# Three fox tiles per chunk in the chunk loop of a two-block transformer kernel, x as the first transfer, and fewer matmul pieces per attention unit

## The chip, the cores and the metric

One core of one Trainium2 chip. The metric is device time in microseconds (us) of one execution. The kernel before takes 821.96 us, the median of 3 runs (821.44 to 823.97).

## The reference, cut to what matters

Two transformer blocks run one after the other on x, 256 tokens of width 1024, all in float32. The change lies in the front half of the first block:

```python
cond = silu(c)
mod = cond @ w_ada + b_ada                    # 6 * 1024 columns
sh1, sc1, g1, sh2, sc2, g2 = split(mod, 6)
h = rms(x, ln1_g) * (1 + sc1) + sh1
u = h @ w_in                                  # 4616 columns
fq, fk, fv, fg, dq, dk, dv = split(u, ...)    # 512, 512, 512, 8, 512, 512, 512 * 2 ...
fox_out  = fox_attention(rms(fq), rms(fk), fv, log_sigmoid(fg + b_f))   # 8 heads of 64
diff_out = diff_attention(rms(dq), rms(dk), dv, lam, slopes)            # 4 heads of 2 x 64
x = x + g1 * (concat(fox_out, diff_out) @ w_out)
```

After it come the feed-forward part of the first block and the whole second block, which the change leaves as they are.

## The kernel before, in words

**One order for all engines.** `plan` (L81) writes out a single list of steps, ORDER. Each engine's program walks that list and executes its own share of each step, in that order, and waits on semaphores for the others. So a step that waits on ScalarE or VectorE holds back everything that stands behind it in the list on that engine. The sync engine (SP) issues the weight transfers from the same list: every `split`, `chunk` and `ada` step has one slab of weights, which lands in one of RAW = 5 slots (L761 to L803). A slot is issued again only when the work on the step five places earlier has freed it (L778 to L786).

**Pieces and splits.** A matmul in float32 is made of three products: a weight slab is cut by a `split` step into a high part (ScalarE, `whi`, L1182) and a low part (VectorE, `wlo`, L1400), and a `piece` is one chunk of 128 rows of the contraction for one tile of 512 output columns: 3 products for each of the 2 token tiles, 6 matmuls (L873 to L875). A tile of `w_in` takes 8 pieces and then an `evac` step: ScalarE copies it out of PSUM (L1335) and, for the first two tiles of fox and of diff, squares it (L1340); VectorE then sums the squares (L1730). There are three fox tiles (q, k, v) and three diff tiles. Where a piece is the first of its slab, `plan` places all splits up to two slabs ahead just before it (L266 to L269).

**The chunk loop.** h can't be made before the adaptive shift and scale are known, so the first part of `w_ada` is taken in 8 chunks of 128 columns for shift and for scale. For chunk j: `rows` (16 matmuls, L916, of the landed chunk with cond), a copy of the row by ScalarE (L1192), `xT` (transposes of the normalised x, L927), `col` (the row turned to columns, 4 entries in a line of the trace, L936), then on VectorE the affine step (L1431, L1432, L1437), and `part0`: high part of h on ScalarE (L1196), low part on VectorE (L1443). Chunk j of h then feeds piece j of every tile of `w_in`. Before the change the loop multiplies two tiles, fox q and fox k, per chunk: the order is piece j of tile 0, `rows` of chunk j+2, piece j of tile 1, then `xT`, `col`, `part0` of chunk j+2 and the split of slab j+2. A slab is 128 rows of 1024 columns. Rows sit in PSUM banks 4 and 5, the transposed x in banks 6 and 7. Fox v follows after the loop as an ordinary tile, behind `fgate` (the forget gates, L1010 to L1013). Then come `logf`, `cum` (L1021) and `heads` 0 (L1034).

**The attention part.** `attention` (L124) writes 8 units here, 4 fox and 4 diff. Unit u puts `scores` of unit u+1 first (L1050, L1058), then `probsT` u (the probabilities transposed, L1079), `heads` u+2, and `values` u (L1109, L1110), and fills the places between them with pieces and `ada` steps (L961, the rest of `w_ada`) from a list called `tail`. BETWEEN (L72) says how many for each place. ScalarE executes the exponentials (L1273), the high parts of the heads (L1264, L1265) and the copies of the transposed probabilities (L1282); VectorE the bias and maximum (L1611, L1612, L1629), the normalisation (L1634 to L1653) and the low parts of the heads (L1588, L1590). The scores of the second head of a unit and the transposed probabilities share PSUM bank 6, so `probsT` u waits for VectorE to have read the scores of u+1.

The places that the change touches:

```python
BETWEEN = {"fox": (2, 1, 2, 1, 2), 1: (2, 1, 2, 1, 1), 2: (3, 1, 1, 0, 1), 3: (2, 0, 2, 0, 1),
           "diff": (2, 0, 1, 0, 1), 7: (1, 0, 1, 0, 2), ...
# unit u: scores u+1, [0] pieces, probsT (u,0), [1] pieces, heads u+2, [2] pieces, probsT (u,1), [3] pieces, values u, [4] pieces
# probsT (u,1) is there for fox units only; [3] likewise
order += [("scores", 0), ("heads", 1), ("lam", 0)] + tail[:3]
```

Of the kernel before, what the change touches and what calls it, by code (L numbers as in the profile page):

```python
# [71 lines left out]
BETWEEN = {"fox": (2, 1, 2, 1, 2), 1: (2, 1, 2, 1, 1), 2: (3, 1, 1, 0, 1), 3: (2, 0, 2, 0, 1),  # L72
           "diff": (2, 0, 1, 0, 1), 7: (1, 0, 1, 0, 2),
# [267 lines left out]
def build(nc, A, out):  # L341

    ctx = ExitStack()
    with ctx:
# [266 lines left out]
        def home(s):  # L611

            return (s // 2 % SPL, s % 2) if s < KC else ((s - KC // 2) % SPL, 0)

        def split_view(t, s):
            slot, half = home(s)
            return t[:, slot, half * 2 * W:half * 2 * W + SLABS[s]["chunks"] * SLABS[s]["cols"]]

# [194 lines left out]
        def _(pe):  # L813
# [41 lines left out]
            for it in ORDER:  # L855
                kind, i = it
                if kind == "piece":
# [1092 lines left out]
```

## Time and profile before

| | us |
|---|---|
| median of 3 runs | 821.96 |
| the profiled execution, its own time | 823.87 |
| span of its trace | 822.1 |
| TensorE (PE) busy | 785.4 |
| VectorE (DVE) busy | 461.3 |
| ScalarE (ACT) busy | 392.6 |
| GpSimd (POOL) busy | 59.2 |

The profiled execution took 1.8 us more than the span of its trace and 1.9 us more than the median. A time in the trace is counted from the span's start. The duration of a matmul in the trace is pipelined (the next starts before it ends), so what a group of matmuls takes is read from the start of one to the start of the next. PEld is the load of the stationary operand, "issue" an idle time for which the profile shows no releaser, and PEclk the granted share of TensorE's clock.

### The profile page before, as it was taken

To read this page: it belongs to the slowest core of one execution; us is meant where nothing else is said; L and a number is where in the kernel's file an instruction comes from. 1 tells how busy PE (TensorE), PEld (TensorE's weight loads), DVE (VectorE), ACT (ScalarE), POOL (GpSimd) and SP (SyncE) were. 2 spreads that over 40 slices of the span, in tenths; PEclk is the share of its full clock that TensorE was granted. 3 is DMA by queue.
4 is the path that set the end of the run, shared out by engine and by line. 5 is a ranking of instruction groups with operands and counts; after the bars stand their busy time and mean duration, and the time that the engine had idled before them with its cause. 6 is when DMAs were issued, how large, how long until landed. Compare 5 with 4: busy or idle time off the path is not lost.

```text
span 822.1 us, 10250 instructions
## 1 busy us (share of the span) xinstructions
PE 785.4 (96%) x3963; PEld 623.7 (76%) x3963; DVE 461.3 (56%) x607; ACT 392.6 (48%) x546; POOL 59.2 (7%) x66
## 2 busy tenths in 40 slices
PE   4898899998999999999999999999999999999995
PEld 2567676566888889788888887777888888888884
DVE  3466676646565556364574445556566565544364
ACT  3255656644344334353644456664464545335252
POOL 2014020000000000000281000000010000000001
PEclk9999999998999999999999999999999999999998
DMA  9997336895555356555758464333555645564601
GB/s 274 294 364 268 104 109 254 335 377 175 196 194 188 122 153 232 202 179 186 255 198 307 154 204 155 103 103 104 159 184 183 184 174 188 174 202 153 202 29 51
DMA packets 86433, 157.67 MB, mean 192 GB/s; under 512 B 5134, under 2 KB 23783, under 8 KB 84338
## 3 DMA queue, kind: packets, MB, share of 16 engines
q1 hardware_dynamic: 84562, 151.16, 55.2%
q0 software_dynamic: 1776, 5.85, 2.3%
q8 instruction: 32, 0.52, 0.3%
q14 instruction: 15, 0.12, 0.0%
q10 hardware_dynamic: 48, 0.01, 0.0%
HBM read 155.94 MB, written 1.07 MB: 191 GB/s over the span
## 4 chain that ended last, share of the span: by engine, by line
PE 85%; DVE 4%; SPq 3%; issue 3%; ACT 2%; DMA 2%; POOL 0%; DVEq 0%; POOLq 0%; ACTq 0%
PE PS L873 25%; PE PS L875 24%; PE PS L874 24%; PE PS L999 2%; DMA raw<-in_w_ada 2%; PE PS L961 1%; PE PS L1109 1%; PE PS L1050 1%; PE PS L1079 1%; ACT whi L1182 1%; SPq L803 1%; DVE wlo L1400 1%; PE PS L1034 1%; SPq L791 1%; SPq L776 1%
## 5 line engine op out<-in xcount | busy, mean ns | idle before, releaser
L1400 DVE TENSOR_TENSOR wlo<-raw,whi 128x2048 fp32r<-128x2048 f32 (+1 forms) x126 | 275.2, 2185 | 197.4 <-ACT whi L1182 170.5
L1182 ACT ACTIVATE whi<-raw 128x2048 fp32r<-128x2048 f32 (+1 forms) x126 | 227.2, 1804 | 154.0 <-PE PS L875 154.0
L873 PE MATMUL PS<-whi,hT 128*128 128x512 f32 (+1 forms) x704 | 280.8, 399 | 2.1 <-issue 1.4
L875 PE MATMUL PS<-whi,hT 128*128 128x512 f32 (+1 forms) x704 | 273.4, 388 | 0.0
L874 PE MATMUL PS<-wlo,hT 128*128 128x512 f32 (+1 forms) x704 | 273.2, 388 | 0.0
L873 PEld LDWEIGHTS PS<-whi,hT 128*128 128x128 f32 x704 | 133.7, 190 | 32.3 <-issue 7.5
L875 PEld LDWEIGHTS PS<-whi,hT 128*128 128x128 f32 x704 | 133.6, 190 | 27.5
L874 PEld LDWEIGHTS PS<-wlo,hT 128*128 128x128 f32 x704 | 134.0, 190 | 24.1
L873 PE MATMUL PS<-whi,hidT 128*128 128x512 f32 x216 | 84.9, 393 | 0.0
L875 PE MATMUL PS<-whi,hidT 128*128 128x512 f32 x216 | 84.1, 389 | 0.0
L874 PE MATMUL PS<-wlo,hidT 128*128 128x512 f32 x216 | 84.1, 389 | 0.0
L874 PEld LDWEIGHTS PS<-wlo,hidT 128*128 128x128 f32 x216 | 40.6, 188 | 8.5 <-issue 0.2
L873 PEld LDWEIGHTS PS<-whi,hidT 128*128 128x128 f32 x216 | 40.6, 188 | 8.5 <-issue 0.2
L875 PEld LDWEIGHTS PS<-whi,hidT 128*128 128x128 f32 x216 | 40.5, 188 | 8.4
L1273 ACT ACTIVATE sc<-sc,nmax 128x128 f32<-128x128 f32 x64 | 28.5, 446 | 33.2 <-DVE nmax L1629 33.0
L1837 POOL TENSOR_TENSOR nss<-nss 128x2 f32<-128x2 f32 x4 | 0.8, 190 | 571.1 <-ACT mod L1172 352.7
L1238 ACT ACTIVATE hidT<-PS 128x512 fp32r<-128x512 f32 x27 | 14.7, 597 | 43.1 <-PE PS L999 43.1
L1540 DVE SCALAR_TENSOR_TENSOR hidT<-PS,hidT 128x512 fp32r<-128x512 f32 x27 | 17.4, 686 | 22.1 <-ACT hidT L1238 22.1
L916 PE MATMUL PS<-raw,cond 128*32 128x256 f32 x128 | 10.3, 447 | 12.5 <-DMA raw<-in_w_ada 12.4
L1365 ACT ACTIVATE hid<-PS 128x1024 f32<-128x1024 f32 x8 | 8.2, 1029 | 24.0 <-PE PS L875 24.0
L1079 PEld LDWEIGHTS PS<-con,sc 128*128 128x128 f32 x84 | 9.9, 140 | 11.4 <-issue 9.4
L1050 PEld LDWEIGHTS PS<-kT,qT 64*128 64x128 f32 x192 | 12.4, 186 | 7.8 <-issue 6.5
(230 smaller groups left out, 669.5 us busy)
## 6 DMA issues: line engine op xcount, KB each, us to landing
raw<-in_w_in SPq DMA_DIRECT2D x36, 1024.0 KB, 5.2
raw<-in_w_ff SPq DMA_DIRECT2D x32, 1024.0 KB, 5.2
raw<-in_w_ada SPq DMA_DIRECT2D x16, 1024.0 KB, 6.4
raw<-in_w_gate SPq DMA_DIRECT2D x10, 1024.0 KB, 5.2
raw<-in_w_up SPq DMA_DIRECT2D x10, 1024.0 KB, 5.1
raw<-in_w_down SPq DMA_DIRECT2D x10, 1024.0 KB, 5.1
raw<-in_w_ada SPq DMA_DIRECT2D x16, 512.0 KB, 7.1
raw<-in_w_out SPq DMA_DIRECT2D x8, 1024.0 KB, 5.0
```

The lines of the kernel that those rows point to most:

```text
L873: pe.matmul(o, ah, wh, start=(k == 0), stop=False)
L874: pe.matmul(o, ah, wl, start=False, stop=False)
L875: return pe.matmul(o, al, wh, start=False, stop=end)
L916: last = pe.matmul(PS[r:r + 32, b, 0:256], cond32[:, k, :], raw[:, slot, k * 256:(k + 1) * 256], start=k < 4, stop=k >= 4)
L999: last = pe.transpose(PS[:, b, o:o + P], src[:, t, c * P:(c + 1) * P], ident)
L1050: last = pe.matmul(PS[:, 5 + n, c0:c1], qT[r, slot, qp, t * P:(t + 1) * P], kT[r, slot, kp, 0:c1 - c0], start=m == 0, stop=m == 2 and not ...
L1079: last = pe.transpose(PS[:, probs_bank(u, n), m * P:(m + 1) * P], src[:, n, c:c + P], ident)
L1182: act.activation(split_view(whi, i), slab_view(raw, slot, i), ACT.Copy).then_inc(hi_made, 1)
L1238: act.activation(hi.rearrange("p c s -> p (c s)"), PS[:, b, :], ACT.Copy, scale=1.0 if gain is None else gain).then_inc(turn_hi, 1)
L1273: act.activation(sc[:, n, c0:c1], sc[:, n, c0:c1], ACT.Exp, bias=nmax[:, a, t:t + 1], scale=-1.0, accum_out=lsum[:, a, t:t + 1]).then_inc( ...
L1400: dve.tensor_tensor(split_view(wlo, i), slab_view(raw, slot, i), whole(split_view(whi, i)), ALU.subtract).then_inc(lo_made, 1)
L1540: dve.scalar_tensor_tensor(out=lo.rearrange("p c s -> p (c s)"), in0=PS[:, b, :], scalar=1.0 if gain is None else gain, in1=hi.rearrange(" ...
```

## The change

The chunk loop multiplies all three fox tiles for each chunk, from slabs of 128 rows by 1536 columns. Fox v has its own two PSUM banks (4 and 5), and the rows move to the banks of the transposed x (6 and 7). `rows` of a chunk now come one chunk ahead of the pieces instead of two: rows j+1, piece j of tile 0, then `xT`, `col`, the split and `part0` of chunk j+1, then piece j of tiles 1 and 2. At the end of the loop the last pieces go tile by tile, so that tiles 0, 1 and 2 are evacuated one after another. `fgate`, `unit` and `logf` follow, and then the whole first diff tile, with one split after its fourth piece, `cum` after the fifth, `heads` 0 after the sixth, and behind its `evac` a split, `scores` 0, `heads` 1 and `lam`. Then two pieces of the second diff tile, and the attention part with 5, 5, 5, 4, 3, 3, 3, 3 pieces in its units, where it had 8, 7, 6, 5, 4, 4, 4, 3. The split buffers are one ring of three slabs from the start. The two small transfers for cond (`crow`, `con`) go from the queue of SP to that of ScalarE, so x is the first that SP issues.

```diff
-BETWEEN = {"fox": (2, 1, 2, 1, 2), 1: (2, 1, 2, 1, 1), 2: (3, 1, 1, 0, 1), 3: (2, 0, 2, 0, 1),
-           "diff": (2, 0, 1, 0, 1), 7: (1, 0, 1, 0, 2),
+BETWEEN = {"fox": (2, 1, 1, 0, 1), 3: (1, 1, 1, 0, 1), "diff": (1, 0, 1, 0, 1),
            "moba": (2, 0, 1, 0, 1), 8: (2, 0, 1, 0, 0), 15: (2, 1, 1, 1, 1)}
...
-    fox = [tile("fox", n, KC, "h") for n in range(2)]
+    fox = [tile("fox", n, KC, "h") for n in range(3)]
...
-    order += [("cond", 0), ("chunk", 0), ("sums0", 0), ("norm", 0), ("rows", 0), ("early", 0), *early, ("xT", 0), *column(0)]
-    order += [*rows(1), ("xT", 1), *early, *column(1)]
+    order += [("cond", 0), ("chunk", 0), ("sums0", 0), ("norm", 0), ("rows", 0), ("early", 0), ("xT", 0), ("col", 0), *early,
+              ("part0", 0)]
     for j in range(KC):
-        slabs.append(dict(weight="w_in", row=j * P, chunks=1, col=0, cols=2 * W))
-        pair = [("piece", dict(T=fox[n], k=j, slab=j, off=n * W, first=n == 0, last=n == 1)) for n in range(2)]
-        if j < KC - 2:
-            order += [pair[0], *rows(j + 2), pair[1], ("xT", j + 2), *column(j + 2), *early]
-            order += {KC - 4: [("setup", 0)], KC - 3: early + [("relbias", 0)]}.get(j, [])
-        elif j == KC - 2:
-            order += [pair[0], *early, ("vectors", 0)]
-            second = pair[1]
+        slabs.append(dict(weight="w_in", row=j * P, chunks=1, col=0, cols=3 * W))
+        step = [("piece", dict(T=fox[n], k=j, slab=j, off=n * W, first=n == 0, last=n == 2)) for n in range(3)]
+        if j < KC - 1:
+            order += rows(j + 1) + step[:1] + [("xT", j + 1), ("col", j + 1), *early, ("part0", j + 1)]
+            if j < KC - 2:
+                order += step[1:]
+                order += [("setup", 0)] if j == KC - 3 else []
+            else:
+                order += [("relbias", 0)]
+                held = step[1:]
         else:
-            order += [pair[0], ("evac", fox[0]), second, pair[1], ("evac", fox[1])]
+            for n in range(3):
+                order += (held[n - 1:n] if n else early + [("vectors", 0)]) + step[n:n + 1] + [("evac", fox[n])]
     order += early + [("fgate", 0), ("unit", 0), ("logf", 0), ("unit", 1)]
-    now = whole("fox", 2, "w_in", 2 * W, "h")
-    order += insert(now, (4, early), (5, [("cum", 0)]), (6, [("heads", 0)]))
     tail = []
     for n in range(3):
         tail += whole("diff", n, "w_in", 3 * W + FOX + n * W, "h")
-    tail = insert(tail, (11, [("unit", 2)]), (20, [("unit", 3)]), (23, ada[8:10]))
+    tail = insert(tail, (4, early), (5, [("cum", 0)]), (6, [("heads", 0)]), (9, early + [("scores", 0), ("heads", 1), ("lam", 0)]),
+                  (11, [("unit", 2)]), (20, [("unit", 3)]), *[(20 + j, [ada[8 + j]]) for j in range(6)])
     wo = [tile("w_out", n, KC, "mix") for n in range(2)]
     fill = slab(wo[0], "w_out", 0, 0) + slab(wo[1], "w_out", W, 0)
-    tail += insert(fill, *[(j, [ada[10 + j]]) for j in range(8)])
-    order += [("scores", 0), ("heads", 1), ("lam", 0)] + tail[:3]
-    tail = tail[3:]
+    tail += insert(fill, *[(2 * j, [ada[14 + j]]) for j in range(4)])
+    ahead = tail.index(("unit", 2))
+    order += tail[:ahead]
+    tail = tail[ahead:]
...
         def home(s):
-            return (s // 2 % SPL, s % 2) if s < KC else ((s - KC // 2) % SPL, 0)
+            return s % SPL
...
         def slabs_under(s):
-            slot, half = home(s)
-            under = [e for e in range(s) if home(e)[0] == slot and (e >= KC or s >= KC or home(e)[1] == half)]
-            return under[-1] + 1 if under else 0
+            return max(0, s - SPL + 1)
...
         def bank0(T):
-            return 2 * (T % 2)
+            return 2 * T if T < 3 else 2 * ((T - 3) % 2)
...
-            sp.dma_start(crow[:, :], A["c"].rearrange("a (r q) -> (a r) q", q=P)).then_inc(cond_in, 16)
-            sp.dma_start(con[:, C_ID:C_ID + P], A["constants"][:, C_ID:C_ID + P]).then_inc(cond_in, 16)
...
-                    b = 4 + i % 2
+                    b = chunk_bank(i)
...
                 elif kind == "xT":
                     b = chunk_bank(i)
-                    take(b)
+                    pe.wait_ge(row_in, i + 1)
...
-                    take(5)
-                    pe.transpose(PS[:, 5, 0:V_ALL], vec[:, :], ident[0:V_ALL, 0:V_ALL]).then_inc(vec_ps, 1)
+                    take(7)
+                    pe.transpose(PS[:, 7, 0:V_ALL], vec[:, :], ident[0:V_ALL, 0:V_ALL]).then_inc(vec_ps, 1)
...
+            act.dma_start(crow[:, :], A["c"].rearrange("a (r q) -> (a r) q", q=P)).then_inc(cond_in, 16)
+            act.dma_start(con[:, C_ID:C_ID + P], A["constants"][:, C_ID:C_ID + P]).then_inc(cond_in, 16)
```

## Rows read from the trace of the kernel before

**Rows 1.** The page: busy time of each engine.
```profile
PE 785.4 (96%) x3963; PEld 623.7 (76%) x3963; DVE 461.3 (56%) x607; ACT 392.6 (48%) x546; POOL 59.2 (7%) x66
```

**Rows 2.** Waits of PE, 0 to 222 us: total us, times, longest.
```profile
PE PS L916 <- DMA raw<-in_w_ada: 12.4, 6, 7.4
```

**Rows 3.** Windows: stretch, us, busy per engine, PEclk, DMA share, GB/s.
```profile
40.00:50.00 10.00, 9.61 (x76) 6.42 (x68) 5.29 (x11) 3.80 (x7) 0.00 (x0) 1.00 1.14 331
50.00:60.00 10.00, 8.62 (x43) 6.43 (x40) 8.07 (x12) 7.30 (x8) 0.45 (x1) 1.00 1.04 386
...
73.30:76.80 3.50, 3.50 (x12) 2.76 (x12) 3.20 (x3) 2.08 (x3) 0.00 (x0) 0.51 0.25 91
```

**Rows 4.** Timeline of chunk steps: start us, us, engine line, operation, idle before.
```profile
34.35 1.07 PE L916 MATMUL PS<-raw,cond 128*32 128x256 f32 x16 [1.47 <-DMA raw<-in_w_ada]
...
44.13 1.07 PE L916 MATMUL PS<-raw,cond 128*32 128x256 f32 x16 [0.22 <-DMA raw<-in_w_ada]
45.13 0.50 PE L873 MATMUL PS<-whi,hT 128*128 128x512 f32 x1
47.20 0.48 PE L873 MATMUL PS<-whi,hT 128*128 128x512 f32 x1
47.76 0.54 DVE L1437 TENSOR_SCALAR aff<-PS,AB 128x256 f32<-128x256 f32 x1
49.01 1.07 PE L916 MATMUL PS<-raw,cond 128*32 128x256 f32 x16 [0.17 <-DMA raw<-in_w_ada]
```

**Rows 5.** Groups by line and form, 10 to 56 us: busy us, mean ns.
```profile
L1400 DVE TENSOR_TENSOR wlo<-raw,whi 128x1024 fp32r<-128x1024 f32 x8 | 9.8, 1226 | 6.7 <-ACT whi L1182 6.7
L1182 ACT ACTIVATE whi<-raw 128x2048 fp32r<-128x2048 f32 x1 | 1.9, 1894 | 0.0
```

**Rows 6.** Timeline, issue of x, end of the loop, the gates.
```profile
1.66 0.43 SPq L763 DMA_DIRECT2D x<-in_x  x1
...
56.03 0.47 PE L873 MATMUL PS<-whi,hT 128*128 128x512 f32 x1 [1.39 <-issue]
...
60.22 2.51 PE L825 MATMUL PS<-hT,wfgs 128*72 128x256 f32 x20
...
62.92 0.19 PEld L873 LDWEIGHTS PS<-whi,hT 128*128 128x128 f32 x1
...
68.17 0.47 DVE L1554 TENSOR_SCALAR fgt<-PS,bf 72x256 f32<-72x256 f32 x1
...
72.60 0.26 PE L1021 MATMUL PS<-con,fgt 8*128 8x8 f32 x2 [2.57 <-DVE fgt L1563]
```

**Rows 7.** Timeline of the first scores, of PE and DVE.
```profile
80.64 0.29 DVE L1611 TENSOR_SCALAR mcum<-con,cumq 128x128 f32<-128x128 f32 x1 [2.68 <-issue]
...
85.44 0.55 PE L1050 MATMUL PS<-kT,qT 64*128 64x128 f32 x6 [0.17 <-DVE kT L1590]
...
90.01 0.28 DVE L1611 TENSOR_SCALAR mcum<-con,cumq 128x128 f32<-128x128 f32 x1
92.52 0.52 PE L1079 MATMUL PS<-con,sc 128*128 128x128 f32 x3 [2.74 <-DVE nmax L1629]
92.96 1.90 ACT L1182 ACTIVATE whi<-raw 128x2048 fp32r<-128x2048 f32 x1
```

**Rows 8.** Timeline of ACT and DVE around the evac of the first diff tile.
```profile
99.27 1.03 ACT L1335 ACTIVATE tok<-PS 128x1024 f32<-128x1024 f32 x1 [2.73 <-PE PS L875]
101.46 1.93 ACT L1182 ACTIVATE whi<-raw 128x2048 fp32r<-128x2048 f32 x1
103.48 2.29 DVE L1400 TENSOR_TENSOR wlo<-raw,whi 128x2048 fp32r<-128x2048 f32 x1 [1.02 <-ACT whi L1182]
```

**Rows 9.** Timeline of a diff unit on DVE and ACT, and the end of attention.
```profile
148.39 0.38 ACT L1300 ACTIVATE tok<-PS 128x256 f32<-128x256 f32 x1 [1.22 <-PE PS L825]
149.32 0.19 ACT L1305 ACTIVATION_READ_ACCUMULATOR sq<-tok 128x1 f32 x1
...
172.38 1.09 PE L999 MATMUL PS<-con,tok 128*128 128x128 f32 x8
```

More of the change, by code:

```diff
@@ L611, in home @@
         def home(s):
-            return (s // 2 % SPL, s % 2) if s < KC else ((s - KC // 2) % SPL, 0)
+            return s % SPL
         def split_view(t, s):
-            slot, half = home(s)
-            return t[:, slot, half * 2 * W:half * 2 * W + SLABS[s]["chunks"] * SLABS[s]["cols"]]
+            return t[:, home(s), 0:SLABS[s]["chunks"] * SLABS[s]["cols"]]
         def slabs_under(s):
-            slot, half = home(s)
-            under = [e for e in range(s) if home(e)[0] == slot and (e >= KC or s >= KC or home(e)[1] == half)]
-            return under[-1] + 1 if under else 0
+            return max(0, s - SPL + 1)
         def landed(eng, it):
@@ L862, in _ @@
                         pe.wait_ge(lo_made, s + 1)
-                    if k == 0 and T >= 2:
-                        for ready in tile_readers(T - 2):
+                    if k == 0 and tile_under(T) >= 0:
+                        for ready in tile_readers(tile_under(T)):
                             pe.wait_ge(*ready)
+                    if (T, k) == (2, 0):
+                        take(4, 5)
                     operand_ready(T, k)
@@ L892, in _ @@
                         last.then_inc(gemm_done, 1)
-                    elif (T, k) == (0, KC - 1):
+                    elif T < 2 and k == KC - 1:
                         last.then_inc(first_done, 1)
+                    if (T, k) == (2, KC - 1):
+                        reader[4] = reader[5] = tile_readers(T)
                 elif kind == "cond":
@@ L935, in _ @@
                     for a in range(2):
-                        last = pe.matmul(PS[:, chunk_bank(i), S + a:S + a + 1], row_of(i)[:, a * P:(a + 1) * P], sel[:, :],
+                        last = pe.matmul(PS[:, chunk_bank(i), a:a + 1], row_of(i)[:, a * P:(a + 1) * P], sel[:, :],
                                          start=True, stop=True)
                     last.then_inc(col_ps, 1)
+                    reader[chunk_bank(i)] = [(aff_made, i + 1)]
                 elif kind == "vectors":
                     pe.wait_ge(vec_in, 16 * NROWS)
-                    take(5)
-                    pe.transpose(PS[:, 5, 0:V_ALL], vec[:, :], ident[0:V_ALL, 0:V_ALL]).then_inc(vec_ps, 1)
-                    reader[5] = [(col_made, 1)]
+                    take(7)
+                    pe.transpose(PS[:, 7, 0:V_ALL], vec[:, :], ident[0:V_ALL, 0:V_ALL]).then_inc(vec_ps, 1)
+                    reader[7] = [(col_made, 1)]
                 elif kind == "relbias":
@@ L950, in _ @@
                     pe.wait_ge(setup_in, 16 * NSETUP)
-                    take(4)
-                    pe.matmul(PS[0:MOBA, 4, 0:SKEW], table[:, :], hot[:, :], start=True, stop=True).then_inc(rel_ps, 1)
-                    reader[4] = [(rel_row, 1)]
+                    take(6)
+                    pe.matmul(PS[0:MOBA, 6, 0:SKEW], table[:, :], hot[:, :], start=True, stop=True).then_inc(rel_ps, 1)
+                    reader[6] = [(rel_row, 1)]
                 elif kind == "ada":
@@ L1430, in _ @@
                     dve.wait_ge(ab0_made, 1 + i)
-                    dve.tensor_scalar(AB[:, 1, i:i + 1], PS[:, b, S:S + 1], col[:, V_B1 + i:V_B1 + i + 1], None, ALU.add)
-                    dve.scalar_tensor_tensor(out=AB[:, 0, i:i + 1], in0=PS[:, b, S + 1:S + 2],
+                    dve.tensor_scalar(AB[:, 1, i:i + 1], PS[:, b, 0:1], col[:, V_B1 + i:V_B1 + i + 1], None, ALU.add)
+                    dve.scalar_tensor_tensor(out=AB[:, 0, i:i + 1], in0=PS[:, b, 1:2],
                                              scalar=col[:, V_B1 + KC + i:V_B1 + KC + i + 1],
@@ L1447, in _ @@
                     dve.wait_ge(vec_ps, 1)
-                    then(dve.tensor_copy(col[:, V_LN2:V_ALL], PS[:, 5, V_LN2:V_ALL]))
+                    then(dve.tensor_copy(col[:, V_LN2:V_ALL], PS[:, 7, V_LN2:V_ALL]))
                     dve.tensor_scalar(col[:, V_ALL:V_ALL + 1], col[:, V_QK:V_QK + 1], HD ** -0.5, None, ALU.mult)
```

19 lines of the change are left out of this document (8 added, 11 removed).

## The prediction
> **What bounds the kernel now.** I read the page's busy times first: TensorE (PE) is busy for 785.4 of 822.1 us [rows 1]. The change adds and removes no matmul, so it can only move the 36.7 us in which PE idles, and the stretches in which its clock is low. The waits of PE show where. In the chunk loop PE waits for chunks of w_ada, 12.4 us in all, of which 7.4 is the first [rows 2]. In the loop's even part a chunk step takes 4.9 us from rows to rows, and PE's work in it ends 0.4 us before the next chunk lands [rows 4]. Behind the loop, PE waits 2.6 us for the forget gates and 2.7 us for the scores of unit 1 [rows 6, 7]. After the first of these waits the granted clock reads 0.51 for 3.5 us (1.2 GHz for 2.4), and after the second it does so again (two such stretches, of which one is shown): about 1.6 us more for each [rows 3].
>
> **The chunk loop.** Three pieces took 4.19 us, so one takes 1.4 [rows 6]. A step before is rows 1.0, two pieces and 0.7 of xT and col: 4.5 us of PE. With a third piece it is 5.9 us [rows 4]. The step's transfers grow from 1.57 to 1.84 MB. The 0.26 MB more take 0.68 us at the 386 GB/s of the stretch in which large slabs flow [rows 3], so the transfers need 5.6 us and PE becomes the bound, narrowly. The bounds of this term: 0.68 us, or 0.82 if all bytes cost what the mixed stream of 40 to 50 us costs (320 to 331 GB/s). The page "DMA: Bandwidth & Descriptors" of the Trainium skill (Specifications) puts line rate at descriptors of 512 B and more, which is what a row of a chunk has; by it all bytes of the step cost alike, 0.82 us, and the loop would end some 0.6 us later. The trace speaks against it: 331 GB/s with chunks in the stream, 386 without [rows 3]. I take 0.68.
>
> x is issued at 1.66 us, behind two small issues; it goes first now, and all behind it on SP comes 0.86 us earlier [rows 6]. Chunk 4, used at 34.35 us before [rows 4], lands 4 x 0.69 later and 0.86 earlier: 36.2. PE, slow at the start as before, has rows 2 at 24.6 and rows 3 at 30.5 by my count, an estimate, and gets there at the same time. Three more steps of 5.9 put rows 7 at 54.1 us, where it stood at 49.0.
>
> The last chunk has no rows behind which its h can be made. From rows 7: the affine step ends after 4.2 (44.13 to 48.30 before, [rows 4]), the low split of 1536 columns takes 1.75 (between 1.23 and 2.29, [rows 5, 8]), the low part of h 0.4: 6.4 us, of which PE can fill 4.5. It waits 1.9 us; before, 1.39 [rows 6]. The remaining five pieces end at 54.1 + 6.4 + 7.0 = 67.5.
>
> **Behind the loop.** fgate takes 2.7, five diff pieces 7.0: PE is at `cum` at 77.1. The chain for cum: ScalarE evacuates fox v until 68.6, the high split 9 ends at 70.5 and the low one at 72.8 [rows 5, 8]. From the first gate operation to cum it takes 4.4 [rows 6]: 77.2. So the wait of 2.6 us goes, and the low clock behind it. What is late next is `unit` 1 before heads 0: 0.4 us. The first diff tile ends at 82.5. Counted in work, this is 7.8 us ahead: before, scores 0 start at 79.1, and eight more pieces (11.2) would end at 90.3.
>
> **The price: scores 1.** Behind the evac of the first diff tile the list now has a split, and only then scores 0. The queues are in order. ScalarE copies and squares (1.8 of the 2.2 us between the evac and the split, [rows 8]), then the high split; the low split starts 2.0 us after the high one and takes 2.2 [rows 8]. VectorE so comes to scores 0 6.3 us after the tile's end, at 88.8. From there to scores 1 on PE it takes 4.8 (80.64 to 85.44, [rows 7]): 93.6. PE has scores 0, heads 1 and two pieces and is done at 87.5. It waits 6 us. Then as before: the split and scores 1 on VectorE, 7.1 us from scores 1 to probsT 0 [rows 7]. That is 100.6 us, in place of 92.52 with seven pieces (9.9 us) fewer done: 1.8 us ahead. The low clock after the wait falls into work that waits anyway; before it cost 1.6 us behind 92.52. So at best 3.4 us are left of 7.8 + 1.6.
>
> **The attention units.** From 92.52 to 172.38 (the diff turns, [rows 7, 9]) are 79.9 us: minus seven pieces (9.9), 1.6 of low clock, 0.8 of waits, leaves 67.6 of work. Fewer pieces cover less of the same chains; unit by unit, from the end of a `scores`:
> - Unit 1: exponentials end after 3.0 (90.01 to 93.0, [rows 7]), evac 1.8, split 1.9, copy 0.4 of the transposed probabilities [rows 8], 7.1; PE has 6.1: waits 1.0.
> - Unit 2: heads copies, split and copy behind heads 4 take 3.5, PE has 2.6: 0.9.
> - Unit 4: the evac of the last diff tile comes before the copy: 0.4.
> - Unit 5: split 16 stands between values 4 and scores 6. ScalarE's share of values takes 1.1 [rows 9], the high split 1.9, the low one 2.2, its four reads of scores 1.2 (half of the eight operations, 2.5 us, of a fox unit, [rows 7]): 6.5 us, against one piece, scores and one piece, 3.9. Wait 2.7 us, as long as both waits that were followed by the low clock: 1.5 more.
>
> Units 0, 3, 6 and 7 cost nothing: there the copies are done before PE asks (margins of 0.3 us and more), and their cover is the piece or `ada` step before `values`. The transfers of the weights cost nothing here: before, PE waited for none behind the loop [rows 2], and the slots come free with splits that are no closer to their use than now; if that cover went, one late slab would cost what is left of its 5 us of transfer. Bounds of the unlisted hand-overs: 0 to 0.3 us in each of eight units; I take 0. Sum: 100.6 + 67.6 + 5.0 + 1.5 = 174.7; with 0.7 for single pieces standing alone (0.1 each between other steps, in more places), 175.4 against 172.38. All behind it is unchanged. **+3.0 us**: the profiled execution would take 823.87 + 3.0 = 826.9, and the median, 1.9 lower, about 825.0. A difference under 0.3% (2.5 us) can't be told from none with this kernel.
>
> **The rivals.**
> 1. *The clock stays up in unit 5 and the waits are as worked out*: +1.5, 823.5 us. For it: the wait before the last chunk's pieces, 1.39 us, was followed by full clock. Against: 2.6 and 2.7 were not. Chance 0.22. Counts as no change.
> 2. *Faster: the units hide their waits.* The head's gain and the wait at scores 1 stand, but the copies and reads of units 1, 2, 4 and 5 come in time, because PE is delayed elsewhere and the chains don't start late. Then 5.0 + 1.5 + 0.7 fall away: -4.2, 817.8; half of it -0.6. It decides where split 16 ends relative to scores 6: VectorE busy for 461 us of 822 [rows 1] has room. Against: every chain above is in order. If VectorE got to scores 0 before 84 us, the 6 us would go too. Chance of being under 819.5: 0.2.
> 3. *The wait of 1.9 us before the last chunk's pieces also lowers the clock*: five pieces and fgate at 1.2 GHz for 3.5 us, +1.4 on top: 826.4. Chance 0.18.
> 4. *The loop stays bound by transfers*, 0.82 us for the larger slab, or the gate weights' tiny transfers delay it as the drop from 6 to 4.9 us steps hints: rows 7 at 55.5, +1.4, 826.4; with rival 3, 827.8. Its opposite, a loop in which the third tile doesn't fill the waits, would show as rows 7 at 49 + 8 x 1.4 = 60, which the step's own times exclude. Chance 0.1.
>
> **How the numbers follow.** The forecast of +3.0 us, 825.0, has 0.3, its own range 823.5 to 826.5. Rivals 3 and 4 lie above it and are slower as well. Rival 1 is within 0.3%, part of the forecast's range too. With 0.2 for rival 2: faster by over 0.3% 0.22, within 0.3% 0.33, slower 0.45. The range runs from 818.5, which takes in most of rival 2, to 828.3, rivals 3 and 4 together.
>
> **What the profile after would show.** Rows 7 (L916) at 54 us in steps of 5.9 with no wait for w_ada behind chunk 4; the last fox piece at 67.5; cum (L1021) without its 2.6 us wait; the first diff tile done at 82.5; then the largest wait of PE outside the first chunk, 6 us before L1050 at about 93.6, released by the low part of kT; probsT at 100.6; a wait of 2.7 us before an L1079 near 153, released by nmax; the diff turns at 175. I am wrong if VectorE starts the mcum of scores 0 before 86 us, if rows 7 comes after 56, or if no wait over 1.5 us stands in units 1 to 7.

## The result and the profile after

The changed kernel takes 826.40 us (median of 6 runs, 825.81 to 828.42); the kernel before, run beside it, 822.11 us (6 runs, 821.44 to 825.02). The ratio is 1.0055, interval 1.0042 to 1.0068: slower by 0.42 to 0.68%. The prediction was 825.0 us, range 818.5 to 828.3, with 0.45 on slower by over 0.3%. The profiled execution took 828.42 us, with a span of 826.7 us where it was 822.1: 4.6 us more, against a forecast of 3.0.

The page's busy times after, beside [rows 1]: PE is busy for 1.1 us more with the same 3963 instructions, so the larger part of the 4.6 us is idle time.

```profile
PE 786.5 (95%) x3963; PEld 624.5 (76%) x3963; DVE 465.2 (56%) x605; ACT 392.8 (48%) x544; POOL 55.1 (7%) x66
```

Where it idles: the waits of PE from 0 to 226 us (total, times, longest), beside [rows 2].

```profile
PE PS L898 <- DMA con<-in_constants: 6.8, 1, 6.8
PE PS L1048 <- DVE kT L1590: 6.0, 1, 6.0
PE PS L916 <- DMA raw<-in_w_ada: 5.7, 3, 2.8
PE PS L1077 <- DVE nmax L1629: 3.5, 2, 2.7
...
PE PS L871 <- DVE hT L1443: 1.7, 1, 1.7
PE PS L1077 <- ACT pt L1282: 1.1, 1, 1.1
```

The waits for w_ada behind chunk 3 and the wait for the forget gates are gone. In their place stand 6.0 us before the scores of unit 1 (L1048), 1.7 us before the last chunk's pieces (L871), and 2.7 us before the transposed probabilities of unit 5 (L1077). The first line is not a loss: PE waits for the identity until 6.8 us instead of 3.1, but the first chunk lands later still, at 9.85 us (10.74 before).

The timeline after, PE, DVE and ACT, from the loop to the end of the diff units (start us, us, engine line, operation, idle before):

```profile
36.69 1.07 PE L916 MATMUL PS<-raw,cond 128*32 128x256 f32 x16
...
54.85 1.07 PE L916 MATMUL PS<-raw,cond 128*32 128x256 f32 x16
...
58.96 1.75 DVE L1400 TENSOR_TENSOR wlo<-raw,whi 128x1536 fp32r<-128x1536 f32 x1
...
61.19 0.76 PE L871 MATMUL PS<-whi,hT 128*128 128x512 f32 x1 [1.75 <-DVE hT L1443]
...
70.97 2.98 PE L821 MATMUL PS<-hT,wfgs 128*72 128x256 f32 x24
...
80.73 0.26 PE L1019 MATMUL PS<-con,fgt 8*128 8x8 f32 x2
...
90.02 2.29 DVE L1400 TENSOR_TENSOR wlo<-raw,whi 128x2048 fp32r<-128x2048 f32 x1 [0.64 <-ACT whi L1182]
92.22 0.28 DVE L1611 TENSOR_SCALAR mcum<-con,cumq 128x128 f32<-128x128 f32 x1
...
97.01 0.90 PE L1048 MATMUL PS<-kT,qT 64*128 64x128 f32 x6 [6.03 <-DVE kT L1590]
...
104.09 0.52 PE L1077 MATMUL PS<-con,sc 128*128 128x128 f32 x3 [0.72 <-DVE nmax L1629]
...
151.26 2.29 DVE L1400 TENSOR_TENSOR wlo<-raw,whi 128x2048 fp32r<-128x2048 f32 x1 [2.35 <-issue]
...
154.81 0.52 PE L1077 MATMUL PS<-con,sc 128*128 128x128 f32 x3 [2.73 <-DVE nmax L1629]
...
177.66 1.09 PE L997 MATMUL PS<-con,tok 128*128 128x128 f32 x8
```

From the first row to the second are three steps of 6.05 us, none with a wait. The low split at 90.02 stands between the first diff tile and the `mcum` of scores 0 (92.22), and PE waits for what comes behind it. The diff turns start at 177.66, where they started at 172.38 [rows 9]: 5.3 us later, 0.7 of which are regained behind them.

The windows of after (stretch, us, busy of PE, PEld, DVE, ACT, POOL, PEclk, DMA share, GB/s) behind the wait of 1.75 us and behind that of 2.73 us:

```profile
61.50:66.00 4.50, 4.50 (x11) 3.46 (x11) 2.59 (x6) 1.87 (x2) 3.22 (x6) 0.50 1.05 386
...
154.81:160.81 6.00, 6.00 (x33) 3.82 (x33) 3.24 (x10) 3.02 (x12) 0.00 (x0) 0.72 0.80 281
```

The granted clock is at its lower level, 1.2 GHz, for all of the first stretch and for a part of the second. The five pieces behind the first wait took 9.8 us (61.19 to 70.97) instead of the 7.0 that they take at 2.4 GHz.

### The profile page after: what moved, and what is told of

Read it like the earlier page. It is cut to its first block, busy times and chain, and to the rows that moved or that the text cites. A ratio compares the mean times of both kernels' runs of the same rounds, so it can differ in the third digit from the quotient of the medians.

```text
span 826.7 us, 10239 instructions
## 1 busy us (share of the span) xinstructions
PE 786.5 (95%) x3963; PEld 624.5 (76%) x3963; DVE 465.2 (56%) x605; ACT 392.8 (48%) x544; POOL 55.1 (7%) x66
## 4 chain that ended last, share of the span: by engine, by line
PE 86%; ACT 3%; DVE 3%; issue 3%; SPq 3%; DMA 1%; POOL 0%; DVEq 0%; POOLq 0%; ACTq 0%
PE PS L871 25%; PE PS L873 24%; PE PS L872 24%; PE PS L997 3%; ACT whi L1182 1%; PE PS L959 1%; PE PS L1048 1%; PE PS L1107 1%; PE PS L1077 1%; DMA raw<-in_w_ada 1%; SPq L799 1%; SPq L772 1%; PE PS L1032 1%; SPq L787 1%; PE PS L916 1%
## 5 line engine op out<-in xcount | busy, mean ns | idle before, releaser
L1400 DVE TENSOR_TENSOR wlo<-raw,whi 128x2048 fp32r<-128x2048 f32 (+2 forms) x124 | 279.9, 2259 | 186.2 <-ACT whi L1182 160.6
L1182 ACT ACTIVATE whi<-raw 128x2048 fp32r<-128x2048 f32 (+2 forms) x124 | 227.0, 1831 | 155.2 <-PE PS L873 152.7
L871 PE MATMUL PS<-whi,hT 128*128 128x512 f32 (+1 forms) x704 | 280.8, 399 | 2.6 <-DVE hT L1443 1.7
L871 PEld LDWEIGHTS PS<-whi,hT 128*128 128x128 f32 x704 | 133.5, 190 | 34.0 <-issue 9.2
L871 PE MATMUL PS<-whi,hidT 128*128 128x512 f32 x216 | 84.9, 393 | 0.0
L871 PEld LDWEIGHTS PS<-whi,hidT 128*128 128x128 f32 x216 | 40.6, 188 | 8.5 <-issue 0.2
L1048 PEld LDWEIGHTS PS<-kT,qT 64*128 64x128 f32 x192 | 13.0, 195 | 13.3 <-DVE kT L1590 7.7
L1048 PE MATMUL PS<-kT,qT 64*128 64x128 f32 (+1 forms) x192 | 16.7, 301 | 6.6 <-DVE kT L1590 6.5
L1077 PEld LDWEIGHTS PS<-con,sc 128*128 128x128 f32 x84 | 9.9, 140 | 11.3 <-issue 9.3
```

Source lines behind the costliest of these rows:

```text
L871: pe.matmul(o, ah, wh, start=(k == 0), stop=False)
L1048: last = pe.matmul(PS[:, 5 + n, c0:c1], qT[r, slot, qp, t * P:(t + 1) * P], kT[r, slot, kp, 0:c1 - c0], start=m == 0, stop=m == 2 and not ...
L1077: last = pe.transpose(PS[:, probs_bank(u, n), m * P:(m + 1) * P], src[:, n, c:c + P], ident)
L1182: act.activation(split_view(whi, i), slab_view(raw, slot, i), ACT.Copy).then_inc(hi_made, 1)
L1400: dve.tensor_tensor(split_view(wlo, i), slab_view(raw, slot, i), whole(split_view(whi, i)), ALU.subtract).then_inc(lo_made, 1)
```

## The experiments

All runs in one table. "Turns" is the start of the diff turns in the profiled execution, clock its mean granted clock. The ratio is the estimate on record, which is not exactly the quotient of the two medians. From the turns to the end are 648.1 to 650.6 us in every profile: the changes act ahead of the turns, and the 2.5 us behind them are scatter between single profiles.

| kernel | median us (runs) | ratio to before, interval | turns | span | clock |
|---|---|---|---|---|---|
| before | 822.11 (6) | | 172.38 | 822.1 | 0.989 |
| after | 826.40 (6) | 1.0055 [1.0042, 1.0068] | 177.66 | 826.7 | 0.985 |
| e3_x_behind | 828.30 (4) | 1.0067 [1.0041, 1.0092] | 177.50 | 826.4 | 0.987 |
| e11_before_x_first | 821.68 (12) | 0.9991 [0.9978, 1.0004] | 171.22 | 820.0 | 0.991 |
| e7_loop_dma | 824.62 (1) | | 173.82 | 822.8 | 0.987 |
| e1_scores_first | 826.00 (10) | 1.0046 [1.0025, 1.0067] | 177.37 | 825.9 | 0.986 |
| e2_split16 | 825.69 (6) | 1.0039 [1.0019, 1.0060] | 173.40 | 824.0 | 0.984 |
| e4_fill_last | 824.09 (10) | 1.0017 [1.0004, 1.0030] | 172.91 | 821.8 | 0.988 |
| e8_splits_ahead | 823.40 (10) | 1.0018 [1.0006, 1.0029] | 174.14 | 823.2 | 0.989 |
| e9_ahead_and_16 | 820.80 (11) | 0.9983 [0.9974, 0.9992] | 171.08 | 819.2 | 0.991 |
| e10_late12 | 820.71 (12) | 0.9986 [0.9978, 0.9995] | 169.23 | 818.4 | 0.990 |
| e12_unit_first | 817.20 (6) | 0.9941 [0.9927, 0.9954] | 167.07 | 815.8 | 0.993 |
| e14_both | 816.78 (6) | 0.9942 [0.9927, 0.9957] | 166.18 | 815.1 | 0.993 |

The kernel before, beside the other runs, took 822.22 (beside e1 to e4), 821.63 (e7 to e10) and 821.66 (e11 to e14).

### x first, by itself: e3 and e11

The changed kernel with the two small transfers ahead of x again, on SP's queue:

```diff
         def _(sp):
+            sp.dma_start(crow[:, :], A["c"].rearrange("a (r q) -> (a r) q", q=P)).then_inc(cond_in, 16)
+            sp.dma_start(con[:, C_ID:C_ID + P], A["constants"][:, C_ID:C_ID + P]).then_inc(cond_in, 16)
...
         def _(act):
-            act.dma_start(crow[:, :], A["c"].rearrange("a (r q) -> (a r) q", q=P)).then_inc(cond_in, 16)
-            act.dma_start(con[:, C_ID:C_ID + P], A["constants"][:, C_ID:C_ID + P]).then_inc(cond_in, 16)
```

> The changed kernel with the two small transfers for cond back on SP's queue ahead of x. Theory: chunk 0 is used at 10.7 in place of 9.85 and all transfers on SP come 0.86 us later; the loop is bound by the transfer of chunk 3 (rows 3 at 30.6, after a wait of 1.3), so rows 7 comes 0.9 us later and the time grows by 0.5 to 0.9 us. Rival (the late landing of con, 6.8 us in place of 3.1, cost as much as the earlier x gains): no difference, or a gain.

The first chunk's rows start at 10.55 us (9.85 in after), the last chunk's pieces at 62.29 (61.19). So the head start of x reaches the end of the loop, and was worth 1.1 us there. In this profile the stretch of low clock behind the 1.75 us wait was shorter (five pieces in 8.5 us, not 9.8), so that the turns came at the same time as in after; the median is 1.9 us higher, more than the expected 0.5 to 0.9, but its interval overlaps with that of after.

The other way round, the kernel before with x first (the same two statements moved from SP to ScalarE):

> This is the kernel before with one part of the change: the two small transfers (c and the identity) go to ScalarE's queue, and x is the first transfer on SP's. Theory A (the chunks of w_ada set the pace of the old loop, so that all of the head start passes through): rows 1 to 7 come 0.9 us earlier, rows 7 at 48.1 us instead of 49.0, the last fox piece, cum and the diff turns follow (171.5), and the median falls by 0.9 us, to 0.9989 of before. Theory B (identity lands late, at 6.8 us, and PE was busy from rows 3 on): rows 7 moves by 0.3 us at most, and the time by nothing that can be told.

Timeline of PE in e11, rows 4 (chunk 4) and 7, then cum:

```profile
33.60 1.07 PE L914 MATMUL PS<-raw,cond 128*32 128x256 f32 x16 [1.47 <-DMA raw<-in_w_ada]
...
48.16 1.07 PE L914 MATMUL PS<-raw,cond 128*32 128x256 f32 x16
...
71.72 0.35 PE L1019 MATMUL PS<-con,fgt 8*128 8x8 f32 x2 [2.58 <-DVE fgt L1563]
```

They are 0.75, 0.85 and 0.9 us earlier than before ([rows 4], [rows 6]): theory A, the loop before ran at the pace of its chunks. The time itself, 0.9991, fits the expected 0.9989 but can't be told from 1. So this part of the change moves the end of the loop by just under a microsecond; that it shortens the whole is not shown.

### Is the new loop bound by PE? e7

The third fox tile computes one of its three products per piece, so the two correction products of v are left out; the transfers stay as they are.

```diff
                         wh = split_view(whi, s)[:, off:off + width]
...
+                        if T == 2:
+                            return pe.matmul(o, ah, wh, start=(k == 0), stop=end)
```

> The changed kernel with one product for fox v in place of three (the high by high one; the two corrections with a low part are left out), so a step of the loop has 3.9 us of PE work fewer by 4 matmuls: about 5.0 us in place of 5.9, with the same transfers. Only the steps of the loop are read. Theory (transfers of a step take 5.6 us, so the loop of the changed kernel is bound by PE, narrowly): the steps from rows 4 to rows 7 take 5.6 us each and PE waits for w_ada in each, about 0.6 us. Rival (the page's line rate, all bytes alike): 5.7 to 5.75 us. Third possibility (transfers had room): under 5.3 us.

Timeline of PE in e7, rows 4 to 7:

```profile
36.69 1.07 PE L918 MATMUL PS<-raw,cond 128*32 128x256 f32 x16 [0.27 <-DMA raw<-in_w_ada]
42.20 1.07 PE L918 MATMUL PS<-raw,cond 128*32 128x256 f32 x16 [0.36 <-DMA raw<-in_w_ada]
47.73 1.07 PE L918 MATMUL PS<-raw,cond 128*32 128x256 f32 x16 [0.36 <-DMA raw<-in_w_ada]
53.18 1.07 PE L918 MATMUL PS<-raw,cond 128*32 128x256 f32 x16 [0.24 <-DMA raw<-in_w_ada]
```

The window over these three steps:

```profile
36.69:53.18 16.49, 15.53 (x108) 10.75 (x108) 8.65 (x16) 7.44 (x10) 0.00 (x0) 1.00 1.13 333
```

With less work on PE each step ends on a chunk of w_ada, and takes 5.50 us (36.69 to 53.18, three steps). That is what the transfers need at the 333 GB/s that this stream reached; the expected 5.6 us was nearly right, and the waits were 0.24 to 0.36 us where 0.6 was expected. The step of after takes 6.05 us without a wait: PE binds it, with 0.55 us to spare.

### Where the wait before scores 1 comes from: e1

The split leaves its place between the first diff tile's evac and scores 0:

```diff
-    tail = insert(tail, (4, early), (5, [("cum", 0)]), (6, [("heads", 0)]), (9, early + [("scores", 0), ("heads", 1), ("lam", 0)]),
+    tail = insert(tail, (4, early), (5, [("cum", 0)]), (6, [("heads", 0)]), (8, [("scores", 0), ("heads", 1), ("lam", 0)]), (9, early),
```

> The changed kernel with scores 0, heads 1 and lam ahead of the evac of the first diff tile and the split behind it. Theory (VectorE's and ScalarE's queues are what limits between the first diff tile and unit 0): VectorE starts scores 0 at about 87.7 us in place of 92.2 and the wait at scores 1 falls from 6.0 to about 1.5 us, but evac and both splits then stand ahead of the reads of scores 1, which start at 101.3 in place of 101.6, so the wait at probsT 0 grows from 0.7 to about 4 us and the time falls by 0.3 us, give or take one stretch of low clock (1.6). Rival (it is the place of that one split that costs): the 4.5 us at scores 1 stay gained, the time falls by 4 us or more.

Timeline of PE in e1:

```profile
90.94 0.55 PE L1048 MATMUL PS<-kT,qT 64*128 64x128 f32 x6 [1.54 <-DVE kT L1590]
...
102.04 0.87 PE L1077 MATMUL PS<-con,sc 128*128 128x128 f32 x3 [5.15 <-DVE nmax L1629]
```

The wait before scores 1 shrinks from 6.03 to 1.54 us, but 5.15 us appear before probsT 0, where there were 0.72. The sum goes from 6.75 to 6.69, and nothing is gained (826.00), as the theory said. The evac and the split that left their place now stand between scores 1 and its reads. From cum to probsT 0 it takes 22.9 us instead of 23.4, and the low clock behind the wait of 5.15 us then takes more than that back: probsT 0 to the turns is 75.3 us instead of 73.6. So the 6 us could not be had by moving these two steps. Is it because DVE has too much to do? The window from cum (80.73) to probsT 0 (104.09) in after:

```profile
80.73:104.09 23.36, 16.35 (x94) 12.66 (x93) 17.71 (x48) 14.18 (x27) 3.27 (x2) 0.85 0.33 107
```

DVE is busy for 17.7 of the 23.4 us, PE for 16.4, part of that at the lower clock. DVE has the most work of the three, but it is not full: for 5.7 us it waits in turn, above all for ACT (2.0 us for the squares of the evac, 0.6 and 1.7 us for the high halves of two splits). The stretch is a chain that runs to and fro between ACT, DVE and PE, and how long it is depends on the order of all its steps.

### The wait in unit 5: e2

One more piece between heads and values of unit 4, one less behind it. Unit 5 so gets split 16 in another place:

```diff
-BETWEEN = {"fox": (2, 1, 1, 0, 1), 3: (1, 1, 1, 0, 1), "diff": (1, 0, 1, 0, 1),
+BETWEEN = {"fox": (2, 1, 1, 0, 1), 3: (1, 1, 1, 0, 1), "diff": (1, 0, 1, 0, 1), 4: (1, 0, 2, 0, 0),
```

> The changed kernel with the piece that brings split 16 ahead of values 4 (unit 4 is 1, 0, 2, 0, 0), nothing else. Theory: ScalarE takes the split before its share of values 4, VectorE reads scores 6 about 2 us earlier against PE, the wait at probsT 5 falls from 2.7 to about 1 us and the low clock behind it (0.5 for some 3.5 us) goes: 3.3 us less, 1.8 if the clock still falls. Rival (a unit with 3 pieces is short of cover wherever they stand): the wait only moves to values 4 or scores 6 and the time stays within 0.5 us.

Timeline of PE in e2 around unit 5, and in the second fence the window behind the wait, columns as above:

```profile
148.89 0.95 PE L1048 MATMUL PS<-kT,qT 64*128 64x128 f32 x12 [0.80 <-issue]
...
152.16 0.52 PE L1077 MATMUL PS<-con,sc 128*128 128x128 f32 x3 [0.72 <-DVE nmax L1629]
```

```profile
152.16:158.16 6.00, 6.00 (x43) 4.20 (x44) 4.13 (x17) 3.58 (x15) 0.00 (x0) 1.00 0.91 326
```

The wait goes from 2.73 to 0.72 us (with 0.80 new before scores 6), and PE issues 43 matmul records in the six microseconds where after had 33, at full clock. The wait and the clock behind it both go, as the prediction had them together. The turns come at 173.40, 4.3 us earlier, of which 1.2 us were there already at cum (79.51 instead of 80.73, less low clock after the loop in this profile); the other 3.1 us are close to the expected 3.3. The median fell by only 0.7 us. That is inside the intervals of either, so what the edit is worth is better read from e8 and e9, which differ by nothing else: 823.40 and 820.80, 2.6 us. The rival (0.5 us at most) doesn't fit that pair.

### The wait before the last chunk's pieces: e4

The first held piece of chunk 6 moves ahead of the first piece of chunk 7:

```diff
-                order += (held[n - 1:n] if n else early + [("vectors", 0)]) + step[n:n + 1] + [("evac", fox[n])]
+                order += ([early + [("vectors", 0)] + held[:1], [], held[1:]][n]) + step[n:n + 1] + [("evac", fox[n])]
```

> The changed kernel with piece 6 of tile 1 ahead of piece 7 of tile 0, so that it fills the wait for the last chunk's h. Theory: of the 1.75 us wait about 0.4 is left, the clock stays at full through the five pieces and the gates (it read 0.50 for 4.5 us), and the first diff tile ends about 3 us earlier; all behind it is a chain, so the time falls by about 3 us (1.4 if the clock falls in any case). Rival (the first diff tile's end is set by the gates' chain on ScalarE and VectorE, not by PE): less than 1 us.

Timeline of PE in e4, and the window behind what is left of the wait:

```profile
60.63 0.47 PE L871 MATMUL PS<-whi,hT 128*128 128x512 f32 x1 [0.30 <-DVE hT L1443]
...
66.20 2.98 PE L821 MATMUL PS<-hT,wfgs 128*72 128x256 f32 x24
...
75.99 0.26 PE L1019 MATMUL PS<-con,fgt 8*128 8x8 f32 x2
```

```profile
60.60:66.60 6.00, 5.97 (x28) 4.97 (x29) 4.18 (x8) 4.08 (x6) 4.15 (x8) 1.00 1.06 381
```

The wait shrinks from 1.75 to 0.30 us and the clock stays up: the four remaining pieces take 5.6 us, 1.39 each. fgate, cum, scores 1 (92.28) and the turns (172.91) all come 4.7 to 4.8 us earlier than in the profile of after. The medians differ by 2.3 us, where 3 were expected. After's profile had a long stretch of low clock here: its five pieces took 9.8 us, those of e1, e3 and e2, behind the same wait, 8.5, 8.5 and 8.3. At 1.2 GHz, the stretch cost 2.8 us in one profile and 1.3 to 1.6 in three.

### Splits where DVE has time: e8, e9, e10

e8 makes splits 8 and 9 around the last chunk's pieces, so that the one between the first diff tile and scores 0 falls away, and fills the wait as e4 does:

```diff
-            for n in range(3):
-                order += (held[n - 1:n] if n else early + [("vectors", 0)]) + step[n:n + 1] + [("evac", fox[n])]
-    order += early + [("fgate", 0), ("unit", 0), ("logf", 0), ("unit", 1)]
+            order += early + [("vectors", 0)] + held + step[:1] + early
+            for n in range(3):
+                order += (step[n:n + 1] if n else []) + [("evac", fox[n])]
+    order += [("fgate", 0), ("unit", 0), ("logf", 0)] + early + [("unit", 1)]
...
-                  ... (9, early + [("scores", 0), ("heads", 1), ("lam", 0)]),
+                  ... (9, [("scores", 0), ("heads", 1), ("lam", 0)]),
```

> The changed kernel with both held pieces ahead of piece 7 of tile 0, split 9 right behind it (ahead of the evacs), split 10 behind logf, split 11 after the fourth diff piece, and no split between the evac of the first diff tile and scores 0: every split after the loop one place earlier. Theory: no wait before piece 7; VectorE starts scores 0 about 3.2 us after the end of the first diff tile in place of 6, so the wait at scores 1 falls from 6.0 to about 2.5 to 3 us, that at probsT 0 grows from 0.7 to about 2.7; the diff turns come at about 170 in place of 177.7, the time falls by 6 us or more against the changed kernel, to 820. Rival (the split is only paid at another place): the gain stays at the 2.3 us that the piece that fills the wait gave.

> The kernel of the splits one place ahead, and split 16 ahead of values 4 as well. Theory: both gains add, the waits at probsT 5 (2.7) and the low clock behind it go: about 3 us below the kernel with the splits ahead alone, near 817 to 818, faster than the kernel before by 4 us. Rival: they don't add, 820.

e9 is e8 with e2's edit. e10 is e9 with split 12 one place later (`min(2, ...)` becomes 1 for slab 10):

> The same with split 12 one place later, behind probsT 0 (both splits 12 and 13 then stand ahead of the fifth piece of the second diff tile). Theory: the wait at probsT 0 (about 2.7 us) goes, and about 1.5 to 2 us of it come back in unit 0, where ScalarE has two splits ahead of heads 2 and of the second probsT's copy: 0.5 to 1 us less than the kernel without it, more if a stretch of low clock goes too. Rival (VectorE's work up to unit 1 is the bound): no difference.

The waits of PE in e8 (0 to 230 us):

```profile
PE PS L1078 <- DVE nmax L1630: 3.9, 2, 2.7
PE PS L1049 <- DVE kT L1591: 3.2, 1, 3.2
PE PS L1033 <- DVE tok L1582: 2.5, 1, 2.5
```

Of the 6.0 us before scores 1, 3.2 are left, but 2.5 have come up before heads 0, and cum to probsT 0 takes 24.4 us, longer than in after. Beside before, e8 (1.0018) is level with e4 (1.0017), which only fills the wait: the expected 820 did not come, and placing the splits elsewhere had again only moved a wait, as the rival said. e9 is the first version under before (0.9983), by what unit 5 cost: 2.6 us below e8, so the gain of e2 adds, but from the higher level of e8 it ends at 820.8 and not at 817 to 818. Split 12 moved nothing in the median (820.71), as its rival said: scores 1 to probsT 0 takes 5.7 us instead of e9's 7.1, but probsT 0 to the turns 71.8 instead of 70.6. The new wait is explained by the timeline of e9:

```profile
76.99 2.29 DVE L1401 TENSOR_TENSOR wlo<-raw,whi 128x2048 fp32r<-128x2048 f32 x1 [1.51 <-ACT whi L1183]
79.19 1.22 DVE L1582 TENSOR_TENSOR tok<-tok,hrs 128x1024 f32<-128x1024 f32 x1
...
80.56 0.89 PE L1033 MATMUL PS<-con,tok 128*128 128x128 f32 x4 [2.49 <-DVE tok L1582]
```

DVE idles for 1.51 us for the high half of the split, then makes the low half, and only then the 1.2 us of unit 1 for which PE waits.

### Unit 1 ahead of the split: e12 and e14

```diff
-    order += [("fgate", 0), ("unit", 0), ("logf", 0)] + early + [("unit", 1)]
+    order += [("fgate", 0), ("unit", 0), ("logf", 0), ("unit", 1)] + early
```

> The kernel of late split 12, with unit 1 ahead of split 10 rather than behind it. It has a wait of 2.5 us before heads 0 (80.4 us), released by the product of unit 1 on VectorE, which stands behind the low split of 2.3 us. Theory A (VectorE's queue as a whole is late here, not the order in it): the wait before heads 0 goes to 0.3 us, but kT of unit 0 then stands behind two low splits, so that about 2 us of wait appear before scores 0; scores 1 moves by less than 0.5 us and the median by less than 0.5 us. Theory B (the place of unit 1 is the cause): 2.1 us earlier from heads 0 on, and the median 2 us lower, about 818.7 beside a before of 821.7 (0.9963).

Timeline of e12:

```profile
76.05 1.22 DVE L1582 TENSOR_TENSOR tok<-tok,hrs 128x1024 f32<-128x1024 f32 x1 [0.25 <-POOL hrs L1804]
77.30 4.49 DVE L1401 TENSOR_TENSOR wlo<-raw,whi 128x2048 fp32r<-128x2048 f32 x2
...
82.72 0.55 PE L1049 MATMUL PS<-kT,qT 64*128 64x128 f32 x6 [1.12 <-DVE kT L1591]
...
89.53 0.55 PE L1049 MATMUL PS<-kT,qT 64*128 64x128 f32 x6 [2.05 <-DVE kT L1591]
```

Unit 1 now fills the time in which DVE had idled, and the wait before heads 0 is gone. As theory A said, kT of unit 0 stands behind two low splits and 1.12 us of wait appear before scores 0, but that is half of what it said; scores 1 comes 2.2 us earlier than in e10 (89.53, not 91.75), its own wait 1.2 us shorter. The window from cum to probsT 0 in e12, to be laid beside that of after in e1's section:

```profile
76.51:95.31 18.80, 15.63 (x94) 12.31 (x93) 16.35 (x51) 11.32 (x26) 3.10 (x2) 0.91 0.32 117
```

DVE is busy for 16.4 of 18.8 us (16.0 of 21.4 in e10): much less of the stretch is idle time of DVE. Theory B holds, and the size is larger than it said: 3.5 us between the medians of e10 and e12, where the spans differ by 2.6. The profiles may well show too little here: in that of e10 the clock stayed up behind the wait before heads 0, while in e8 and e9 the same wait was followed by 1.2 GHz (last section); how often it fell in the other runs of e10 was not recorded.

e14 has in addition scores 0 ahead of the evac of the first diff tile (`(8, ...)` in place of `(9, ...)`):

> As the last one, and scores 0 stands ahead of the evac of the first diff tile, whose VectorE and ScalarE parts then come behind the exponentials. Theory A: the chain to scores 1 starts 2.3 us sooner and the wait of 3.3 us before it shrinks to about 1, but the evac then stands between scores 1 and its reads, so that 1.5 to 2.5 us of wait come before probsT 0; the median moves by less than 0.8 us. Theory B: both waits are only matters of order, and the median falls by 4 us, to about 816.7 (0.994).

Timeline of PE in e14, scores 1 and probsT 0:

```profile
88.41 0.55 PE L1049 MATMUL PS<-kT,qT 64*128 64x128 f32 x6 [1.55 <-DVE kT L1591]
...
94.37 0.52 PE L1078 MATMUL PS<-con,sc 128*128 128x128 f32 x3
```

The wait before scores 1 is 1.55 us in place of 2.05, and the median 0.4 us lower, less than the intervals can tell. Nearly all of theory B's 4 us came from e12's part; for the place of scores 0, theory A's bound (under 0.8 us) holds. Its wait before probsT 0 doesn't show: the clock was low behind scores 1, and the two pieces there took 4.6 us (89.75 to 94.37) where two take 2.8 at full clock, which would cover such a wait. With three tiles in the loop the last two kernels take 0.994 of before and 0.988 of after (816.78 / 826.40). How much of this is due to the third tile is not shown, since no run gives the kernel before a better order of its splits and units.

## Why the prediction was right

The direction, the range and the largest new wait were right; the rise was 4.3 us (median) or 4.6 (profile), not 3.0.

- **The loop.** Predicted rows 7 at 54.1 us, came 54.85. The steps are 6.05 us, not 5.9: the piece that follows other work takes 1.52 us (43.74 to 45.26), the others 1.4. That makes 0.45 us in three steps; the other 0.3 was there at rows 4 (36.69, not 36.4). That the loop passes from its transfers to PE was right. By e7 the transfers of a step need 5.50 us, so the third tile's bytes cost 0.6 us over the old 4.9, below both bounds of the term (0.68 and 0.82). The rule of the Trainium skill that spoke for 0.82 (page "DMA: Bandwidth & Descriptors", Specifications: line rate from 512 B upwards) would have made the transfers 5.7 us a step, still under 6.05: it would have changed the margin only. The trace doesn't agree with it: the stream with the chunks' rows of 512 B moved 333 GB/s in e7, that without chunks 386 [rows 3]; that the size of the rows is the reason is not shown. Rival 4 is refuted: rows 7 came before its 55.5 us, with no wait for a transfer behind chunk 3.
- **The last chunk.** Its wait was predicted at 1.9 us and came as 1.75, the low split of 1536 columns at 1.75 exactly.
- **The clock behind that wait: the step that was mis-sized.** The forecast held that the clock would stay up, because it had behind 1.39 us [rows 6]; rival 3 had it fall, with a chance of 0.18. It fell, in all five profiles that have the wait (after, e1, e2, e3, e7), and stayed up where the wait was 1.38 (e11) or 0.30 us (e4): what rival 3 describes is what happened. It cost 2.8 us in after and 1.3 to 1.6 in e1, e2 and e3, where rival 3 allowed 1.4. With 0.75 us from the loop this gives the 3.5 us by which fgate is late (70.97 instead of 67.5), and these 3.4 to 3.6 us are all that scores 1 (97.01, not 93.6) and probsT 0 (104.09, not 100.6) are off.
- **The price at scores 1.** Predicted at 6 us, released by the low part of kT, came as 6.03. The stretch from cum to probsT 0 was predicted at 23.5 us and took 23.4. What the text did not say is whether moving the split would help; e1 showed that it doesn't.
- **The units.** Waits of 1.0, 0.9, 0.4 and 2.7 us were predicted, and 1.10, 0.60, 0.26 and 2.73 came. Rival 1 (clock up in unit 5) is refuted for this kernel: after, e1, e3, e4, e7 and e8, all with the wait of 2.73 us, read a granted clock of 0.50 in a 2 us stretch within 4 us of its end; e2, e9 and e12, with 0.72, stay at 1.00. From probsT 0 to the turns 74.8 us were predicted, 73.6 came: 1.2 us too many. The waits of units 2 and 4 are 0.4 of it; the rest may lie in the 0.7 for single pieces and in the clock's 1.5, which no run separates. That hides a third of the error ahead, by luck.
- **Rival 2** (the units hide their waits, 817.8) did not happen. e12 and e14 end near its number, at 817.2 and 816.8, but by other means: they also fill the wait of the last chunk and shorten the one at scores 1, which rival 2 left standing.

In sum: +0.75 (loop) +2.8 (clock) −1.2 (units) on the forecast's 3.0 is the 5.3 us at the turns. That the median rose by 4.3 us and ended at 826.40, exactly rival 3's number, is luck: it takes the loop's error and the units' error to cancel in part. Of the 7.8 us by which the forecast had PE ahead behind the first diff tile, 4.1 were there (scores 0 at 86.21 with eight more pieces done, where before, from 79.14, they would end at 90.3); the loop and the clock had taken the rest. 6.0 were then lost at scores 1, since the chain over DVE and ACT ahead of it did not get shorter: from cum to probsT 0 PE took 19.9 us before and 23.4 after, where DVE was busy for 14.3 and 17.7.

## What to carry to other kernels

Work that is pulled forward into a transfer-bound loop is taken from behind it, where it covered something: take the chain over the slower queues (here splits, evacs and units on ACT and DVE) between two points, their work and the time in which they wait for each other, and compare it with what is left on PE between them. If the chain is longer, moving one step on it may only move the wait (e1, e8); what helped was a short step put into the time in which DVE waited for ACT (e12). Between the loop and the turns, most waits of PE of 1.5 us and more were paid twice, as idle time and again at half clock (1.3 to 2.8 us more behind a wait of 1.75), unless a further wait followed: fill such waits first.

## What the runs showed of the hardware

- From the end of the loop to the turns, the thirteen profiles have 30 waits of PE between 1.54 and 6.09 us, and 28 were followed by 1.2 GHz, among them 1.54 us (e1), 1.55 (e14), 1.75, 2.05 (e12), 2.58 (e11) and 2.73. Waits of 0.30, 0.72, 1.38 and 1.39 us were not. The length of the wait alone doesn't decide it. In the loop, the granted clock stayed at 1.00 behind waits of 1.76 (e12) and 3.37 us (e7, before rows 3). And the same wait is not always followed by the same: that of 2.7 us before probsT 0 was followed by 1.2 GHz in before and not in e11. Its line in e11 and the window behind it:

```profile
93.01 0.52 PE L1077 MATMUL PS<-con,sc 128*128 128x128 f32 x3 [2.72 <-DVE nmax L1629]
```

```profile
93.01:99.01 6.00, 6.00 (x32) 5.03 (x33) 4.31 (x8) 4.31 (x8) 0.00 (x0) 1.00 0.45 149
```

That of 2.5 us before heads 0 was followed by it in e9 and not in e10, whose order and timing are equal up to there. The window behind it in e9 (first fence) and in e10 (second):

```profile
80.60:82.60 2.00, 2.00 (x8) 1.71 (x9) 2.00 (x2) 0.84 (x2) 0.00 (x0) 0.55 0.77 295
```

```profile
80.60:82.60 2.00, 2.00 (x12) 1.69 (x12) 2.00 (x3) 0.84 (x2) 0.00 (x0) 1.00 0.85 332
```

The first diff tile so ends 1.7 us earlier in e10 (its evac starts at 83.85 us, not 85.56). A single profile of such a kernel is uncertain by this much, which is why the medians move less smoothly than the turns in the table.

- A small transfer that was issued behind x, on another queue, came late. The identity, issued on ScalarE's queue at 1.44 us, was there at 6.8; issued on SP's queue ahead of x at 1.25 us, it was there at 3.1 (before); e3, with the same order, has it at 3.2. Whether the queue or the place behind x does it was not separated. Timeline of after:

```profile
0.79 0.43 SPq L759 DMA_DIRECT2D x<-in_x  x1
...
1.44 0.36 ACTq L1159 DMA_DIRECT2D con<-in_constants  x1
...
6.81 0.27 PE L898 MATMUL PS<-con,crow 8*128 8x8 f32 x1 [6.81 <-DMA con<-in_constants]
```

- A step's transfers of 1.84 MB in 5.50 us are 334 GB/s (e7), where the step before moved 1.57 MB in 4.9 us, 321 GB/s: with wider rows of w_in beside the chunks the stream was slightly faster. The cause was not tested.
